# Recurrent layer of a decoder step: gate units issued behind the previous head's matrices, copied out by VectorE, silu in place

## The chip, the cores and the metric

The kernel runs on one core of a Trainium2 chip. The metric is the device time of one execution in microseconds (us). The core has five engines with queues of their own: TensorE (PE, matmuls, which land in eight PSUM banks), VectorE (DVE), ScalarE (ACT), GpSimd (POOL) and SyncE (SP, here the issuer of the DMAs). They meet at semaphores; each engine works through its own list strictly in order.

## The reference, cut to what matters

One inference step of a two-layer decoder, 512 prompt tokens and 32 sample tokens (8 sequences of 4), model width 1024, all float32. Layer 0 is a gated linear recurrence with 8 heads of 128, layer 1 is attention; each is followed by a mixture of experts. The change is in layer 0 alone:

```python
def hgrn2_mixer(hn, w_in, lb, gnorm_w, w_o, s0):
    proj = hn @ w_in                              # 1024 x 4096
    q, f, i, g = jnp.split(proj, 4, axis=-1)
    fg = lb + (1.0 - lb) * jax.nn.sigmoid(f)
    logf, k = jnp.log(fg), 1.0 - fg
    o, s_new = gla_chunked(heads(silu(q)), heads(k), heads(i), heads(logf), s0)
    o = rmsnorm(o, gnorm_w).reshape(B, T, A_WIDTH) * jax.nn.silu(g)
    return o @ w_o, s_new
```

`gla_chunked` carries a 128 x 128 state through the tokens: decayed products of q and k inside a chunk, q times the carried state, and the state's update from k and i. The gate `g` enters only at the very end, as `silu(g)` times the gain `gnorm_w`.

## The kernel before

The program is a row of stages with a barrier between them. `hgrn_block` is the stage of the change. It holds i as `hgrn_v` and g as `hgrn_g`, by tokens: five token tiles of 128, 128, 128, 128 and 32 rows. A **unit** is one projection into one PSUM bank:

- `v` units, ten of them (two halves of 512 columns by five token tiles), ahead of everything else;
- `g` units, the **gate units**, numbered 0 to 9 in the same way (half n // 5, token tile n % 5). Units 4 and 9 are the tiles of 32 rows. A unit of 128 rows is eight matmuls of 512 columns (L404), one of 32 rows is 32 matmuls of 128 columns (L407);
- `f` and `q` units of a head, by feature, eight matmuls each (L774); and for every second head an `s` unit (L407), f and q of the sample tokens for two heads, which ScalarE copies out (L522) and TensorE transposes (L833).

All units but `s` take banks 0 and 1 in turn, in the order in which they are issued. `begin(u)` lets TensorE wait until the unit that had the bank before has been read out. `f` is read out by ScalarE's sigmoid (L527, L529), `q` by its silu (L533, L534), a gate unit by its silu (L541).

The heads follow each other in software pipeline. For head h the engines do this:

- VectorE and ScalarE, function `elementwise` and `exponentials`: the logarithm (L546), a prefix sum (L632), and for seven levels i = 0 to 6 differences (L649, L650, L655), their exponential (ScalarE L560) and the products with q (VectorE L672) and with k (GpSimd L736, the last one L740, called kd here). Level i + 1's differences need level i - 1's products, so the three engines hand each level on to each other.
- TensorE, function `gla(h)`: transposes of kd (L787), six sets of masked products (L794, each read out by VectorE L682), the state's steps, and the output of the head into banks 7 and 6, the last of which are the matmuls of L817. It begins with waits for all products of head h. ScalarE's copy of the output (L569) is the first thing behind `gla(h)` and ahead of the next logarithm (L546), because in ScalarE's list `results(h)` stands before `exponentials(h + 1)`.

In TensorE's list the order is: f and q of head h, the gate units of head h, then `gla(h - 1)`. ScalarE's list has for head h: read out f and q, silu of the gate units, `results(h - 1)`, `exponentials(h)`. The split of gate units over the heads is a table:

```python
GATE_UNITS = [[("g", n // NT, n % NT) for n in range(*span)] for span in ((0, 2), (2, 3), (3, 4), (4, 5), (5, 6), (6, 7),
                                                                          (7, 8), (8, 8), (8, 10))]
```

So head 0 has two gate units, heads 1 to 6 one each, head 7 none, and two follow between `gla(6)` and `gla(7)`. VectorE multiplies all ten units of `hgrn_g` with the gain (L718) after `elementwise(7)` and ahead of `matrices(7)`, the reading out of `gla(7)`.

The weights of the gate come in two tiles of 2 MB, through a ring of three slots; the second one may be loaded once gate unit 4 is done, since it takes the first one's slot.

## Time and profile before

| | us |
|---|---|
| median of 3 runs | 1665.6 (1656.18 to 1666.4) |
| the profiled execution, whole | 1667.51 |
| its span, first to last instruction | 1665.8 |
| TensorE busy in the span | 1347.6 (81%) |
| VectorE, ScalarE, GpSimd busy | 744.7, 392.9, 170.4 |

The profiled execution took 1.7 us more than its span, and 1.9 us more than the median of the other runs. Busy time is a share over all stages; the stage of the change runs from about 36 to 463 us of the span, and its pipeline of heads from 101 to 461 us. Mean granted clock of TensorE is 0.897 of full speed.

### The profile page before, as it was taken

How to read it: one execution, taken by the hardware profiler on the slowest of the kernel's cores; microseconds unless marked ns; L12 is line 12 of the kernel's file. 1: busy time of each engine (PE TensorE's matmuls, PEld its weight loads, DVE VectorE, ACT ScalarE, POOL GpSimd, SP SyncE). 2: the span in 40 equal slices, each digit the busy share in tenths (PEclk: the TensorE clock that was granted, in tenths of full speed). 3: DMA queues.
4: the chain of work that ended last, by engine and by line, in shares of the span. 5: the costliest groups of instructions: out<-in, count | busy, mean ns of one | idle time of the engine just before them, and what ended most of it. 6: DMA issues, size and time to landing. Idle time of an engine off the chain costs nothing. (4 is left out here: it accounts for less than half of the span.)

```text
span 1665.8 us, 29086 instructions
## 1 busy us (share of the span) xinstructions
PE 1347.6 (81%) x11207; PEld 766.3 (46%) x11207; DVE 744.7 (45%) x1874; ACT 392.9 (24%) x1070; POOL 170.4 (10%) x242
## 2 busy tenths in 40 slices
PE   3998888888679999971999986678778689999880
PEld 2444555455445765541454543344444245765540
DVE  4314465446756331115110454688887156321115
ACT  2013333333321121112001120244444211121111
POOL 1002222222200100002000000100100000100002
PEclk9999999999789799995999988799899789799995
DMA  5140314112371699953131649999999771699924
GB/s 206 51 133 0 116 56 157 65 56 67 115 254 51 227 366 364 335 199 107 58 115 51 245 167 349 364 407 398 398 406 366 280 262 51 234 365 352 327 63 161
DMA packets 132156, 347.56 MB, mean 209 GB/s; under 512 B 22012, under 2 KB 51887, under 8 KB 123824
## 3 DMA queue, kind: packets, MB, share of 16 engines
q1 hardware_dynamic: 115652, 315.21, 52.3%
q0 software_dynamic: 4992, 17.83, 3.0%
q10 hardware_dynamic: 11372, 12.62, 2.4%
q8 instruction: 92, 1.51, 0.4%
q14 instruction: 48, 0.39, 0.1%
HBM read 302.09 MB, written 43.52 MB: 207 GB/s over the span
## 5 line engine op out<-in xcount | busy, mean ns | idle before, releaser
L404 PE MATMUL bank<-wring,xT 128*128 128x512 f32 x512 | 242.0, 632 | 24.6 <-ACT gla_fin L527 16.1
L404 PEld LDWEIGHTS bank<-wring,xT 128*128 128x128 f32 x512 | 102.2, 203 | 153.8 <-issue 132.5
L1304 PE MATMUL bank<-wring,xT 128*128 128x512 f32 x256 | 119.3, 619 | 2.0 <-DVE xT L1224 2.0
L774 PE MATMUL bank<-xT,wring 128*128 128x512 f32 x256 | 111.9, 595 | 0.0
L2301 DVE STREAM_TRANSPOSE wring<-wring 128x1024 f32<-128x1024 f32 x64 | 77.3, 1228 | 41.8 <-DMA wring<-cache_k 41.3
L2301 DVE STREAM_TRANSPOSE attn_q_xT<-attn_q_xT 128x1024 f32<-128x1024 f32 x64 | 77.0, 1227 | 32.2 <-DMA attn_q_xT<-cache_k 32.0
L1304 PEld LDWEIGHTS bank<-wring,xT 128*128 128x128 f32 x256 | 49.3, 199 | 59.4 <-issue 59.3
L682 DVE COPY_PREDICATED gla_att<-level_masks,bank 128x512 f32<-128x512 int32 x48 | 35.1, 730 | 92.2 <-PE bank L794 92.2
L774 PEld LDWEIGHTS bank<-xT,wring 128*128 128x128 f32 x256 | 48.1, 190 | 59.3 <-issue 59.3
L1937 PE MATMUL bank<-attn_q_xT,wring 128*128 128x512 f32 x128 | 56.9, 597 | 0.0
L794 PE MATMUL bank<-gla_qe,gla_ke 128*128 128x128 f32 x384 | 52.5, 295 | 4.7 <-DVE gla_att L682 4.7
L794 PEld LDWEIGHTS bank<-gla_qe,gla_ke 128*128 128x128 f32 x384 | 49.2, 206 | 7.7 <-DVE gla_att L682 7.0
L1511 DVE TENSOR_TENSOR hgrn_g<-hgrn_g,bank 128x128 f32<-128x128 f32 x32 | 7.8, 284 | 83.4 <-ACT hgrn_g L1460 83.4
L1511 DVE TENSOR_TENSOR attn_qo<-attn_qo,bank 128x128 f32<-128x128 f32 x32 | 7.8, 284 | 83.4 <-ACT attn_qo L1460 83.4
L560 ACT ACTIVATE gla_diff<-gla_diff 128x512 f32<-128x512 f32 (+1 forms) x48 | 30.3, 632 | 60.6 <-DVE gla_diff L650 51.5
L2156 PE MATMUL bank<-ident,attn_k 128*128 128x128 f32 x80 | 16.5, 330 | 34.5 <-DVE attn_k L2293 34.5
L2217 PE MATMUL bank<-wring,sa_at 128*32 128x512 f32 x224 | 38.4, 818 | 7.1 <-DMA wring<-cache_v 7.0
L329 PE MATMUL bank<-ident,attn_k 128*128 128x128 f32 (+1 forms) x40 | 6.5, 323 | 46.1 <-DVE attn_k L384 43.5
L732 POOL TENSOR_TENSOR gla_ke<-gla_k,gla_diff 128x544 f32<-128x544 f32 x8 | 10.8, 1345 | 297.8 <-ACT gla_diff L555 297.8
L2417 ACT ACTIVATE attn_k<-attn_k,pa_stat 128x128 f32<-128x128 f32 (+2 forms) x64 | 35.3, 555 | 25.0 <-DVE pa_stat L2284 25.0
L736 POOL TENSOR_TENSOR gla_ke<-gla_k,gla_diff 128x256 f32<-128x256 f32 x40 | 34.9, 871 | 42.3 <-ACT gla_diff L560 42.3
L1467 ACT ACTIVATE moe_norm_w<-bank 128x512 f32<-128x512 f32 x32 | 19.1, 597 | 84.6 <-PE bank L1615 84.6
(425 smaller groups left out, 2355.6 us busy)
## 6 DMA issues: line engine op xcount, KB each, us to landing
wring<-cache_k SPq DMA_DIRECT2D x64, 512.0 KB, 7.0
attn_q_xT<-cache_k SPq DMA_DIRECT2D x64, 512.0 KB, 8.0
xT<-cache_v SPq DMA_DIRECT2D x60, 512.0 KB, 7.7
wring<-cache_v SPq DMA_DIRECT2D x56, 512.0 KB, 6.3
moe_wd<-moe_w_down SPq DMA_DIRECT2D x20, 1024.0 KB, 13.8
wring<-moe_w_gate SPq DMA_DIRECT2D x18, 1024.0 KB, 13.0
wring<-moe_w_up SPq DMA_DIRECT2D x18, 1024.0 KB, 15.5
wring<-a_w_in SPq DMA_DIRECT2D x16, 1024.0 KB, 8.9
```

Of the source, the lines that this page charges most:

```text
L404: last = nc.tensor.matmul(bank[:, :], xT[:, c, cols(t)], w[:, c, :], start=(c == 0), stop=(c == DC - 1))
L560: nc.scalar.activation(diff[i % 2][:, 0:w], diff[i % 2][:, 0:w], ACT.Exp).then_inc(exp_ready, 1)
L682: nc.vector.copy_predicated(A[:, :, :], bcast(k.levelmask[:, i, :].bitcast(I32), 1, [P, PT, P]), k.ps[3 + i % 2][:, :].rearrange("p (c n) ...
L736: nc.gpsimd.tensor_tensor(blocks(KE[j][:, :], size)[:, :, lo], blocks(kk[:, 0:SEQ], size)[:, :, lo], blocks(diff[j % 2][:, 0:SEQ], size)[: ...
L774: last = nc.tensor.matmul(bank[:, :], lhsT, k.xT[:, c, 0:SEQ], start=(c == 0), stop=(c == DC - 1))
L794: last = nc.tensor.matmul(k.ps[3 + i % 2][:, part], KE[i][:, part], QE[i][:, part], start=True, stop=True)
L1304: last = nc.tensor.matmul(bank[:, :], k.xT[:, c, cols(t)], w[:, c, :], start=(c == 0), stop=(c == DC - 1))
L1467: nc.scalar.activation(self.YW[u][:, :], k.ps[5][:, :], ACT.Copy).then_inc(self.y_a, 1)
L1937: last = nc.tensor.matmul(k.ps[2 + h % 2][:, :], w[h // 4][:, c, (h % 4) * P:(h % 4 + 1) * P], self.q_xT[:, c, 0:SEQ], start=(c == 0), sto ...
L2217: last = nc.tensor.matmul(VALUE[n][QUAD * r:QUAD * (r + 1), :], AT[:, p, :], keys.values(v_s)[:, r, n * HB:(n + 1) * HB], start=(g == 0), ...
L2301: nc.vector.transpose(page, page).then_inc(keys_turned, 1)
L2417: last = nc.scalar.activation(part, part, ACT.Exp, bias=s[:, x, 2 + c:3 + c], accum_out=s[:, x, 4 + c:5 + c])
```

## The change

It does four things. In TensorE's list `gla(h - 1)` moves ahead of the gate units of head h. A gate unit is read out of its bank by VectorE, with a plain copy (`gate_out`) that stands inside `elementwise(h)`, behind the products of level i = 4; ScalarE's silu then runs in place on the copy in SBUF, one head later (`gate`), and VectorE's product with the gain (`gate_norm`) follows `elementwise` of that later head, unit by unit, instead of all ten in one go. And the table gives head 6 no gate unit and head 7 three: units 7, 8 and 9.

```diff
-GATE_UNITS = [[("g", n // NT, n % NT) for n in range(*span)] for span in ((0, 2), (2, 3), (3, 4), (4, 5), (5, 6), (6, 7),
-                                                                          (7, 8), (8, 8), (8, 10))]
+GATE_UNITS = [[("g", n // NT, n % NT) for n in range(*span)] for span in ((0, 2), (2, 3), (3, 4), (4, 5), (5, 6), (6, 7), (7, 7), (7, 10))]
 GATE_TILE_AT = [0, 4]
+GATES_AFTER = 4
...
             order += [("f", h), ("q", h)] + GATE_UNITS[h]
-        order += GATE_UNITS[HEADS]
...
                 def gate(u):
-                    done, bank = units[u]
                     _, i, t = u
-                    act.wait_ge(proj_done, done)
-                    for n, (src, dst) in enumerate(token_parts(k.ps[bank], g, i, t)):
-                        last = nc.scalar.activation(dst, src, ACT.Silu)
-                    last.then_inc(g_out, 1)
+                    act.wait_ge(*evacuated[u])
+                    part = g[0:rows(t), t, i * HB:(i + 1) * HB]
+                    nc.scalar.activation(part, part, ACT.Silu).then_inc(g_ready, 1)
...
                 for h in range(HEADS):
                     evacuate_qf(h)
-                    for u in GATE_UNITS[h]:
-                        gate(u)
                     if h:
+                        for u in GATE_UNITS[h - 1]:
+                            gate(u)
                         results(h - 1)
                     exponentials(h)
-                for u in GATE_UNITS[HEADS]:
+                for u in GATE_UNITS[HEADS - 1]:
                     gate(u)
...
+                def gate_out(u):
+                    done, bank = units[u]
+                    dve.wait_ge(proj_done, done)
+                    for src, dst in token_parts(k.ps[bank], g, u[1], u[2]):
+                        last = nc.vector.tensor_copy(dst, src)
+                    last.then_inc(g_out, 1)
+
+                def gate_norm(u):
+                    _, i, t = u
+                    dve.wait_ge(g_ready, NT * i + t + 1)
+                    gv = g[0:rows(t), t, i * HB:(i + 1) * HB].rearrange("p (h n) -> p h n", n=P)
+                    nc.vector.tensor_tensor(gv, gv, bcast(gnorm[0:rows(t), :], 1, [rows(t), 4, P]), ALU.mult)
...
                                                     blocks(diff[j % 2][:, 0:SEQ], size)[:, :, up], ALU.mult).then_inc(q_lev, 1)
+                        if i == GATES_AFTER:
+                            for u in GATE_UNITS[h]:
+                                gate_out(u)
...
                 for h in range(1, HEADS):
                     matrices(h - 1)
                     elementwise(h)
-
-                for i in range(2):
-                    for t in range(NT):
-                        dve.wait_ge(g_out, NT * i + t + 1)
-                        gv = g[0:rows(t), t, i * HB:(i + 1) * HB].rearrange("p (h n) -> p h n", n=P)
-                        nc.vector.tensor_tensor(gv, gv, bcast(gnorm[0:rows(t), :], 1, [rows(t), 4, P]), ALU.mult)
+                    for u in GATE_UNITS[h - 1]:
+                        gate_norm(u)
                 matrices(HEADS - 1)
+                for u in GATE_UNITS[HEADS - 1]:
+                    gate_norm(u)
...
+                    if h:
+                        gla(h - 1)
                     for u in GATE_UNITS[h]:
                         by_token(u, w_gate)
-                    if h:
-                        gla(h - 1)
-                for u in GATE_UNITS[HEADS]:
-                    by_token(u, w_gate)
                 gla(HEADS - 1)
```

What the change does to the lists is seen best in the built program. First TensorE, from f and q of head 1 to f and q of head 2, before. The names: `wring` is the ring of weights, `xT` the normed input, a number behind `bank` is the PSUM bank; `gla_inv4` holds kd, L817 is the last line of `gla`.

```order
L774 MATMUL bank0<-xT,wring2 128x512 x8
L774 MATMUL bank1<-xT,wring2 128x512 x8
L404 MATMUL bank0<-wring0,xT 128x512 x8
L787 MATMUL bank5<-ident,gla_inv4 128x128 x4
...
L817 MATMUL bank6<-gla_s0_0,gla_qb 32x128 x8
L407 MATMUL bank2<-wring1,xT 32x128 x32
L774 MATMUL bank1<-xT,wring1 128x512 x8
L774 MATMUL bank0<-xT,wring1 128x512 x8
```

The same stretch of TensorE's list after the change, where L785 is the former L774, L798 the former L787 and L828 the former L817:

```order
L785 MATMUL bank0<-xT,wring2 128x512 x8
L785 MATMUL bank1<-xT,wring2 128x512 x8
L798 MATMUL bank5<-ident,gla_inv4 128x128 x4
...
L828 MATMUL bank6<-gla_s0_0,gla_qb 32x128 x8
L404 MATMUL bank0<-wring0,xT 128x512 x8
L407 MATMUL bank2<-wring1,xT 32x128 x32
L785 MATMUL bank1<-xT,wring1 128x512 x8
L785 MATMUL bank0<-xT,wring1 128x512 x8
```

The gate unit (L404) has moved from ahead of `gla(0)` to behind it, and keeps bank 0; q of head 2, the last row, still follows it in bank 0.

Second, VectorE's list in the last head, from the products of level 4 to the reading out of `gla(7)`, before:

```order
L672 TENSOR_TENSOR gla_qe<-gla_q,gla_diff 128x16x16
L649 TENSOR_TENSOR gla_diff<-gla_b 128x4x64
L650 TENSOR_TENSOR gla_diff<-gla_b 128x4x64
L672 TENSOR_TENSOR gla_qe<-gla_q,gla_diff 128x8x32
L655 TENSOR_TENSOR gla_diff<-gla_b 128x512
L655 TENSOR_TENSOR gla_diff<-gla_b 128x32
L672 TENSOR_TENSOR gla_qe<-gla_q,gla_diff 128x4x64
L675 COPY gla_qb<-gla_qs 128x8x4
L718 TENSOR_TENSOR hgrn_g<-hgrn_g,row_gains 128x512 x4
L718 TENSOR_TENSOR hgrn_g<-hgrn_g,row_gains 32x512
...
L682 COPY_PREDICATED gla_att<-level_masks,bank 128x512 x6
```

The same after the change (L682 is the former L672, L695 the former L682, L659, L660 and L665 the former L649, L650 and L655):

```order
L682 TENSOR_TENSOR gla_qe<-gla_q,gla_diff 128x16x16
L621 COPY hgrn_g<-bank 128x512 x2
L621 COPY hgrn_g<-bank 32x128 x4
L659 TENSOR_TENSOR gla_diff<-gla_b 128x4x64
L660 TENSOR_TENSOR gla_diff<-gla_b 128x4x64
L682 TENSOR_TENSOR gla_qe<-gla_q,gla_diff 128x8x32
L665 TENSOR_TENSOR gla_diff<-gla_b 128x512
L665 TENSOR_TENSOR gla_diff<-gla_b 128x32
L682 TENSOR_TENSOR gla_qe<-gla_q,gla_diff 128x4x64
L688 COPY gla_qb<-gla_qs 128x8x4
L695 COPY_PREDICATED gla_att<-level_masks,bank 128x512 x6
```

The ten products with the gain are gone from ahead of the reading out, and six copies out of PSUM stand in the middle of the levels.

Third, TensorE's end of the pipeline, from f and q of head 7 on, before:

```order
L774 MATMUL bank<-xT,wring 128x512 x16
L787 MATMUL bank<-ident,gla_inv 128x128 x4
...
L817 MATMUL bank<-gla_s_0,gla_qb 32x128 x8
L404 MATMUL bank<-wring,xT 128x512 x8
L407 MATMUL bank<-wring,xT 32x128 x32
L787 MATMUL bank<-ident,gla_inv 128x128 x4
```

and after:

```order
L785 MATMUL bank<-xT,wring 128x512 x16
L798 MATMUL bank<-ident,gla_inv 128x128 x4
...
L828 MATMUL bank<-gla_s_0,gla_qb 32x128 x8
L404 MATMUL bank<-wring,xT 128x512 x16
L407 MATMUL bank<-wring,xT 32x128 x32
L798 MATMUL bank<-ident,gla_inv 128x128 x4
```

Between the last two `gla` stand three gate units instead of two.

## Rows read from the trace of the kernel before

**Rows 1.** Windows view, the pipeline of heads; busy us per engine, TensorE's clock, DMA.

```profile
101.00:461.30 360.30, 306.14 (x1504) 182.97 (x1500) 186.19 (x322) 127.84 (x251) 86.61 (x72) 0.91 0.27 89
```

**Rows 2.** Timeline of TensorE, heads 2 and 3; start, duration, in brackets idle before.

```profile
192.91 10.19 PE L404 MATMUL bank<-wring,xT 128*128 128x512 f32 x16 [1.58 <-ACT gla_fin L527]
202.94 0.60 PE L787 MATMUL bank<-ident,gla_inv 128*128 128x128 f32 x4
...
216.59 14.00 PE L774 MATMUL bank<-xT,wring 128*128 128x512 f32 x32
236.91 3.46 PE L407 MATMUL bank<-wring,xT 128*32 128x128 f32 x64 [6.32 <-ACT gla_fin L527]
```

**Rows 3.** Timelines of ScalarE, VectorE and GpSimd after `gla(1)`.

```profile
216.70 0.60 ACT L569 ACTIVATE hgrn_v<-bank 128x512 f32<-128x512 f32 x1 [12.27 <-PE bank L817]
...
230.68 0.41 DVE L672 TENSOR_TENSOR gla_qe<-gla_q,gla_diff 128x256 f32<-128x256 f32 x1
...
235.09 1.33 POOL L740 TENSOR_TENSOR gla_inv<-gla_k,gla_diff 128x544 f32<-128x544 f32 x1 [0.88 <-ACT gla_diff L560]
```

**Rows 4.** Timeline of ScalarE, copies of a head's output: heads 0, 5, 6, 7.

```profile
172.53 0.60 ACT L569 ACTIVATE hgrn_v<-bank 128x512 f32<-128x512 f32 x1 [12.28 <-PE bank L817]
...
384.23 0.60 ACT L569 ACTIVATE hgrn_v<-bank 128x512 f32<-128x512 f32 x1 [12.28 <-PE bank L817]
...
419.39 0.60 ACT L569 ACTIVATE hgrn_v<-bank 128x512 f32<-128x512 f32 x1 [12.30 <-PE bank L817]
...
461.34 0.60 ACT L569 ACTIVATE hgrn_v<-bank 128x512 f32<-128x512 f32 x1 [19.99 <-PE bank L817]
```

**Rows 5.** Timeline of TensorE, gate units 8 and 9 behind `gla(6)`.

```profile
419.29 7.13 PE L404 MATMUL bank<-wring,xT 128*128 128x512 f32 x16
426.35 1.96 PE L407 MATMUL bank<-wring,xT 128*32 128x128 f32 x64
```

**Rows 6.** Timeline of VectorE, copies of `v` units out of PSUM.

```profile
97.51 0.69 DVE L617 COPY hgrn_v<-bank 128x512 f32<-128x512 f32 x1 [6.17 <-PE bank L404]
99.43 1.18 DVE L617 COPY hgrn_v<-bank 32x128 f32<-32x128 f32 x4 [1.22 <-PE bank L407]
```

**Rows 7.** Timelines of TensorE, ScalarE and VectorE in head 0.

```profile
128.72 13.90 PE L774 MATMUL bank<-xT,wring 128*128 128x512 f32 x32
...
117.19 0.19 ACT L534 ACTIVATE gla_q<-bank 128x32 f32<-128x32 f32 x1
...
129.53 1.28 ACT L546 ACT_TABLE_LOAD   x1
130.83 0.66 ACT L546 ACTIVATE gla_fin<-gla_fin 128x544 f32<-128x544 f32 x1
...
142.71 0.41 DVE L672 TENSOR_TENSOR gla_qe<-gla_q,gla_diff 128x256 f32<-128x256 f32 x1
```

**Rows 8.** TensorE behind short waits (timeline), and its clock (windows: ..., clock, DMA, GB/s).

```profile
52.23 15.70 PE L404 MATMUL bank<-wring,xT 128*128 128x512 f32 x32 [2.30 <-DVE hgrn_v L617]
...
1106.29 1.95 PE L2183 MATMUL bank<-wring,sa_q 128*32 128x128 f32 x64 [1.64 <-DVE sa_red L2310]
...
192.90:199.10 6.20, 6.19 (x8) 2.57 (x9) 0.00 (x0) 2.02 (x4) 3.07 (x2) 0.50 0.00 0
```

**Rows 9.** Timelines of TensorE and VectorE, `gla(6)` and `gla(7)`.

```profile
404.05 1.09 PE L787 MATMUL bank<-ident,gla_inv 128*128 128x128 f32 x4 [5.93 <-POOL gla_inv L740]
439.27 1.08 PE L787 MATMUL bank<-ident,gla_inv 128*128 128x128 f32 x4 [10.96 <-POOL gla_inv L740]
...
448.65 5.53 PE L794 MATMUL bank<-gla_qe,gla_ke 128*128 128x128 f32 x32 [4.67 <-DVE gla_att L682]
...
437.30 10.66 DVE L718 TENSOR_TENSOR hgrn_g<-hgrn_g,row_gains 128x512 f32<-128x512 f32 x10
```

**Rows 10.** Source view of L718 (ns min/median/max), DMA view (KB each, us to landing).

```profile
L718 DVE TENSOR_TENSOR hgrn_g<-hgrn_g,row_gains x10: 672/674/2397, 437.3 to 447.3; 128x512 f32<-128x512 f32 x8, 32x512 f32<-32x512 f32 x2
...
wring<-a_w_in SPq DMA_DIRECT2D x8, 1024.0 KB, 9.1
```

More of the change, by code:

```diff
@@ L482, in hgrn_block @@
         proj_done, s_copied, s_turned = k.sem("proj_done"), k.sem("sample_qf_copied"), k.sem("sample_qf_turned")
-        v_out, qf_out, g_out = k.sem("v_evacuated"), k.sem("qf_evacuated"), k.sem("g_evacuated")
+        v_out, qf_out, g_out, g_ready = k.sem("v_evacuated"), k.sem("qf_evacuated"), k.sem("g_evacuated"), k.sem("g_ready")
         evacuated = {}
```

## Prediction, made before the changed kernel had run

> **What bounds the kernel now.** I read the windows first, then the chain of work around one head. The pipeline of heads takes 360.3 us, and TensorE is busy for 306.1 of them [rows 1]; it is the busiest engine by far, and idles 54 us. The timeline of TensorE shows where: after f and q of head 3 it stands still for 6.32 us until ScalarE's sigmoid has read f out of its bank (L527), because the gate unit wants that bank; only then come the gate unit and `gla(2)` [rows 2]. ScalarE is late since the exponentials of head 2 stand ahead of that sigmoid. So the loop of a head is serial: end of `gla`, levels, sigmoid, gate unit, next `gla`.
>
> I count from a mark M, the start of ScalarE's copy L569, which is released by the last matmul of `gla`. After M = 216.70 the products of level 4 end at 231.09, M + 14.4; kd starts at 235.09 and ends at M + 19.7 [rows 3]. With kd everything is there that `gla` needs: in the one head without a gate unit, `gla(6)` starts at 404.05, which is M + 19.8 behind the mark of 384.23 [rows 4, 9]. `gla` itself lasts 13.8 us when the clock is at full speed (202.94 to 216.70 [rows 2, 3]), and 15.3 when TensorE comes to it from a wait (404.05 to 419.39 [rows 4, 9]). Before, a gate unit of 7.1 to 10.2 us [rows 2, 5] lay between M + 19.8 and `gla`. The marks run from 172.53 for head 0 to 461.34 for head 7 [rows 4], 41.3 us a head.
>
> **The change, part by part.** *Gate units behind `gla`.* TensorE now goes from `gla(h - 1)` straight into the gate unit of head h, then s, f and q of head h + 1, while VectorE, ScalarE and GpSimd work through the levels. Prices at full clock: f or q 7.0 (two in 14.00 [rows 2]), gate unit 7.1 [rows 5] (7.0 here), small gate unit or s unit 1.9 [rows 5]. TensorE starts 0.1 ahead of M. The wait for the sigmoid goes: f of head h is read out while `gla(h - 1)` runs.
>
> *What is late next* is the bank. q of head h + 1 takes the bank of the gate unit of head h, which VectorE now frees behind level 4. A copy of 128 x 512 out of PSUM takes 0.69, the four copies of a small unit 1.18 [rows 6]. The bank is free at M + 14.4 + 0.7 = M + 15.1, or M + 15.6 for the small unit.
>
> Heads by their lists, TensorE's time from mark to mark:
> - Marks 1 to 2 and 3 to 4 (gate, f, q): f ends at M + 13.9, q waits to 15.1 and ends at 22.1; `gla` 13.8 makes 35.9 each.
> - Marks 0 to 1 and 4 to 5 (gate, s, f, q): f ends at 15.8, so no wait; q ends at 22.8, the transpose of L833 adds 0.3; 36.9 each.
> - Mark 2 to 3 (small gate, s, f, q): f ends at 10.7, q waits to 15.6, 4.9 idle. Behind such waits the clock falls to the lower level, 1.2 GHz: 0.50 from 192.9 to 199.1 [rows 8]. The price is 1.7 (15.70 for work that takes 14.0, behind a wait of 2.30 [rows 8, 2]) to 3.1 (the gate unit of 10.19 against 7.1 [rows 2, 5]); I take 2.4. Sum 15.6 + 7.0 + 2.4 + 0.3 + 13.8 = 39.1.
> - Mark 5 to 6 (f, q, no gate): limited by the levels as before, 419.39 - 384.23 = 35.2 [rows 4].
> - Mark 6 to 7: gate units 7 and 8 end at M + 13.9. Unit 9 needs unit 7's bank, free at 15.1, and ends at 17.05. VectorE stands in the middle of its levels until then, and its four copies end at 18.25: the levels resume 3.85 later than at M + 14.4. `gla(7)` starts at 19.8 + 3.85 = 23.65, from a wait, so 15.3: 39.0.
>
> Together 258.9 from mark 0 to mark 7, against 288.8 before: 29.9 less.
>
> *Head 0.* `gla(0)` comes ahead of gate unit 2, and ScalarE no longer holds the logarithm back for two silus of gate units. Before, L546 loads its table at 129.53 and starts at 130.83; now the table (1.28) follows the silu of q, which ends at 117.38, so the logarithm starts at 118.7 and all levels 12.1 earlier [rows 7]. Level 4's product ends at 143.1 - 12.1 = 131.0, the first gate bank is free at 131.7. TensorE is through with both gate units at about 128.8 (f of head 1 started at 128.72), so it now waits 2.9 us where it did not; f and q take 14.0 plus 1.7 for the clock, to 147.4. `gla(0)` ends at 161.2 instead of 172.5: 11.3 less. All in all 41.2 less, with mark 7 near 420.1.
>
> *The end.* The ten products with the gain (10.66 us on VectorE) no longer stand ahead of the reading out of `gla(7)`, for which TensorE waited 4.67 [rows 9]; that is inside the 39.0. Three of them now follow `matrices(7)` at 0.67 each [rows 10], 2.0 in all. `matrices` ends with L706, for which TensorE has long issued what it needs: it still has the whole output of the head to do (L810 to L817), which covers them; without that cover they cost 2.0.
>
> *Work that is merely moved.* ScalarE's silus in place stand between the silu of q and the transposed kd's copy; `gla` needs that copy only behind its six sets of products, which are the larger part of its 13.8 us, so one or two silus are covered. The second gate tile's load waits for gate unit 4, now done 1.9 behind mark 2, and TensorE asks for it ahead of `gla(3)`, at about M + 25; a load takes 9.1 to land [rows 10], twice that still fits. SyncE's later loads and stores move with the marks. The number of table loads stays.
>
> *Two places where a price has two ends.* The waits of 1.2 us ahead of q (two heads), and of 1.15 ahead of unit 9: behind 1.64 us of waiting, 64 matmuls took 1.95, the full-clock time of rows 5, and behind 2.30 us the clock had fallen [rows 8]. I take no loss; if it falls there, 1.7 to 3.1 for each. The Trainium skill ("TensorE: Matmul & The Clock Gate", "What's actually happening") has the activity monitor free-running, not started by the kernel, so that the same wait may or may not cost the clock. By it two or three such waits would give back some 5 us more; the rows with 1.64 and 2.30 neither confirm nor rule that out.
>
> The products with the gain now run just as GpSimd does kd and its two next operations. Ten took 10.66 where ten times 0.67 is 6.7, and one took 2.397 [rows 9, 10]: I read that as waiting for GpSimd. If they hold kd back in turn, by 0.67 to 1.4 per head, `gla` could start at M + 20.5 + 1.4 = 21.9, still ahead of q's end at 22.1; I take nothing. The Trainium skill ("SBUF — State Buffer", "Who interferes with whom") says that a VectorE instruction with two SBUF inputs and a GpSimd instruction that reads SBUF block each other fully, whichever starts first. That speaks against putting them side by side; by it kd is late in six heads, but behind q.
>
> **The rivals.** *The levels become the bound.* With the copy (0.7) and blocked products of up to 2.4 us ahead of or beside kd, kd ends at M + 19.7 + 0.7 + 2.4 = 22.8, and with the port taken twice at 24. Five heads lose 1 to 2 us: 5 to 10 us given back, 1629 to 1634. For it: L718's 2.397. Against: L740 is the first of GpSimd's three operations, and VectorE's products with the gain come behind all its own levels, so mostly GpSimd is first.
>
> *The clock gives back what the order gains.* TensorE goes cold at all short waits: two heads, unit 9 and a longer spell in head 0 and mark 2 to 3: 3 x 3.1 + 1.4 + 0.7 = 11, so 1636.
>
> *Slower: the bank of the gate unit.* TensorE is strictly in order, and q of head h + 1 waits for VectorE's copy; behind q stands `gla(h)`, behind that the next levels. A head costs copy's end + 7.0 + 13.8. It equals the former 41.3 when the copy ends at M + 20.5, 5.4 later than computed; at M + 23 every head costs 2.5 us more than before, and the five heads concerned with the other terms unchanged give about 1675. That would need level 4 itself to be that late; nothing in rows 3 moves it, since its inputs come from ScalarE and GpSimd, which lose nothing ahead of it.
>
> *The change does not do what it says:* some wait that I missed keeps TensorE where it was, and only head 0 and the end gain: 1650. The built order speaks against it.
>
> **How the numbers follow.** The profiled execution was 1667.5; less 41.2 gives 1626.3. Against the median of the runs, 1665.6, it gives 1624.4, and I forecast 1624. Nothing behind the stage depends on absolute time; the stages behind it move forward as a whole. The runs before spread over 10 us, so a change of under 1% can't be told from none. Chances: forecast (1615 to 1629) 0.62; levels 0.12; clock 0.14; only part of it, 1640 to 1650, 0.06; slower 0.03; better than computed, below 1615 (a fast draw like 1656.18, or less cold clock), 0.03. The range takes in the first four cases but the tails: 1612 to 1640. Faster by over 1% is below 1649: 0.92; within 1% 0.05; slower 0.03.
>
> **What would show it.** Right: marks 35 to 39 us apart; TensorE goes on into the gate unit without a wait behind `gla`; a wait of about 1 us ahead of q, released by L621; `gla(7)` without a wait for VectorE in its middle; mark 7 near 420. Wrong: `gla` released by kd in most heads, gate units or q at 10 us, or L621 at M + 20.

## The result, and the profile after

The changed kernel takes 1617.55 us (median of 5 runs, 1615.37 to 1626.92) against 1664.99 us before (1656.18 to 1666.4, 5 runs). The ratio is 0.9723, with a 95% interval of 0.9694 to 0.9752. The forecast was 1624 with a range of 1612 to 1640, so time and direction came as forecast. The middle was 6.5 too high; that is within what the medians of one kernel do here, since the same changed kernel has 1624.55 in its second session (e11, below), where the gain over before is 40.4 and not 47.4.

The profiled execution of the changed kernel took 1626.92 us (span 1625.2, mean granted clock 0.909), 40.6 less than the profiled one before. First the marks, from the timeline of ScalarE: heads 0, 2, 3, 5 and 7, the rows that answer to [rows 4]. L566 is the former L569.

```profile
158.36 0.60 ACT L566 ACTIVATE hgrn_v<-bank 128x512 f32<-128x512 f32 x1 [11.22 <-PE bank L828]
...
230.69 0.60 ACT L566 ACTIVATE hgrn_v<-bank 128x512 f32<-128x512 f32 x1 [11.75 <-PE bank L828]
...
270.07 0.60 ACT L566 ACTIVATE hgrn_v<-bank 128x512 f32<-128x512 f32 x1 [10.24 <-PE bank L828]
...
342.40 0.60 ACT L566 ACTIVATE hgrn_v<-bank 128x512 f32<-128x512 f32 x1 [10.23 <-PE bank L828]
...
417.54 0.60 ACT L566 ACTIVATE hgrn_v<-bank 128x512 f32<-128x512 f32 x1 [13.66 <-PE bank L828]
```

With those of heads 1, 4 and 6 (194.92, 305.85 and 378.86) the seven distances are, beside the forecast:

| us | head 0 | 0-1 | 1-2 | 2-3 | 3-4 | 4-5 | 5-6 | 6-7 | mark 7 |
|---|---|---|---|---|---|---|---|---|---|
| before | 172.53 | 44.17 | 37.42 | 42.66 | 43.57 | 43.88 | 35.16 | 41.95 | 461.34 |
| forecast | 161.2 | 36.9 | 35.9 | 39.1 | 35.9 | 36.9 | 35.2 | 39.0 | 420.1 |
| changed | 158.36 | 36.56 | 35.77 | 39.38 | 35.78 | 36.55 | 36.46 | 38.68 | 417.54 |

Mark 7 came 43.8 earlier, and the span is shorter by 40.6. What follows the mark took 1204.5 before and 1207.7 here. That part is the same program, and in all the profiled executions of this study it took between 1198.0 and 1210.9 (two executions of one and the same kernel: 1198.0 and 1207.5). Its granted clock is 0.89 in both kernels, and TensorE is busy in it for 970.5 us before and 971.4 us after. The 3 us are left open, as a draw of those stages.

Second, the pipeline's windows, the view of [rows 1], over the stretch of before, which now holds 44 us of the next stage too, and over the pipeline alone:

```profile
101.00:461.30 360.30, 327.87 (x1608) 194.82 (x1607) 210.87 (x421) 133.91 (x269) 88.02 (x82) 0.95 0.35 117
...
101.00:417.60 316.60, 292.96 (x1499) 176.71 (x1497) 187.30 (x338) 125.34 (x245) 86.44 (x72) 0.97 0.31 101
```

TensorE idled 54.2 of 360.3 us before; now it idles 23.6 of 316.6. So 30.6 of the 43.7 us are idle time that is gone. The other 13.2 are its own work, 306.1 to 293.0 us. Of that 0.9 is work that now lies ahead of 101 us, since the pipeline starts 1.0 earlier; the other 12.2 are the same matmuls in less time: the clock in the stretch rose from 0.91 to 0.97.

Third, the waits view of TensorE from 101 to 418 us, with all that it lists there (total, times, longest):

```profile
PE bank L798 <- POOL gla_inv L751: 12.2, 2, 6.3
PE bank L785 <- DVE hgrn_g L621: 10.2, 4, 5.0
PE bank L407 <- DVE hgrn_g L621: 1.1, 1, 1.1
```

None of the waits for the sigmoid (L527, L529) or for the samples' copy (L522) is left; that copy stood for 8.5 us in the same view of before, which the prediction didn't name, though its lists rightly have no such wait. What stands there now is the pair that the prediction named: the copy L621 ahead of q, and kd (L751, the former L740) in the last two heads. Last, TensorE's timeline around `gla(1)` and `gla(2)` and at the last head. This answers to [rows 2] and [rows 9]; L785 is the former L774, L798 the former L787.

```profile
130.76 14.00 PE L785 MATMUL bank<-xT,wring 128*128 128x512 f32 x32 [2.85 <-DVE hgrn_g L621]
...
201.78 7.03 PE L785 MATMUL bank<-xT,wring 128*128 128x512 f32 x16
209.96 7.13 PE L785 MATMUL bank<-xT,wring 128*128 128x512 f32 x16 [1.15 <-DVE hgrn_g L621]
...
246.22 10.13 PE L785 MATMUL bank<-xT,wring 128*128 128x512 f32 x16 [5.01 <-DVE hgrn_g L621]
...
362.59 1.08 PE L798 MATMUL bank<-ident,gla_inv 128*128 128x128 f32 x4 [6.30 <-POOL gla_inv L751]
363.68 8.02 PE L805 MATMUL bank<-gla_qe,gla_ke 128*128 128x128 f32 x48
...
393.90 1.96 PE L407 MATMUL bank<-wring,xT 128*32 128x128 f32 x64 [1.15 <-DVE hgrn_g L621]
401.79 1.09 PE L798 MATMUL bank<-ident,gla_inv 128*128 128x128 f32 x4 [5.94 <-POOL gla_inv L751]
...
402.89 7.49 PE L805 MATMUL bank<-gla_qe,gla_ke 128*128 128x128 f32 x48
```

The forecast waits were 1.2, 4.9, 2.9 (head 0) and 1.15 (ahead of unit 9); the rows have 1.15, 5.01, 2.85 and 1.15. The six sets of masked products of `gla(7)` (L805 at 402.89) have no wait for VectorE in their middle.

### The profile page after: what moved, and what is told of

Its sections match the earlier page's. It is cut to its first block and busy times, and to the rows that moved or that the text cites. A ratio compares the mean times of both kernels' runs of the same rounds, so it can differ in the third digit from the quotient of the medians.

```text
span 1625.2 us, 29095 instructions
## 1 busy us (share of the span) xinstructions
PE 1337.0 (82%) x11207; PEld 763.4 (47%) x11207; DVE 745.8 (46%) x1890; ACT 391.1 (24%) x1064; POOL 168.7 (10%) x242
## 5 line engine op out<-in xcount | busy, mean ns | idle before, releaser
L404 PE MATMUL bank<-wring,xT 128*128 128x512 f32 x512 | 227.8, 602 | 5.0 <-PEq L359 4.4
L404 PEld LDWEIGHTS bank<-wring,xT 128*128 128x128 f32 x512 | 96.9, 192 | 124.6 <-issue 123.2
L785 PE MATMUL bank<-xT,wring 128*128 128x512 f32 x256 | 115.6, 609 | 10.2 <-DVE hgrn_g L621 10.2
L1313 PE MATMUL bank<-wring,xT 128*128 128x512 f32 x256 | 120.4, 624 | 2.0 <-DVE xT L1233 2.0
L785 PEld LDWEIGHTS bank<-xT,wring 128*128 128x128 f32 x256 | 49.0, 194 | 73.3 <-issue 59.8
L1313 PEld LDWEIGHTS bank<-wring,xT 128*128 128x128 f32 x256 | 49.8, 201 | 60.1 <-issue 60.0
L695 DVE COPY_PREDICATED gla_att<-level_masks,bank 128x512 f32<-128x512 int32 x48 | 35.1, 731 | 61.3 <-PE bank L805 61.3
L805 PE MATMUL bank<-gla_qe,gla_ke 128*128 128x128 f32 x384 | 51.8, 293 | 0.0
L805 PEld LDWEIGHTS bank<-gla_qe,gla_ke 128*128 128x128 f32 x384 | 48.7, 205 | 2.9 <-DVE gla_att L695 2.4
L2192 PE MATMUL bank<-wring,sa_q 128*32 128x128 f32 x1024 | 32.2, 279 | 6.3 <-DVE sa_red L2319 6.3
```

The lines of the kernel that those rows point to most:

```text
L404: last = nc.tensor.matmul(bank[:, :], xT[:, c, cols(t)], w[:, c, :], start=(c == 0), stop=(c == DC - 1))
L695: nc.vector.copy_predicated(A[:, :, :], bcast(k.levelmask[:, i, :].bitcast(I32), 1, [P, PT, P]), k.ps[3 + i % 2][:, :].rearrange("p (c n) ...
L785: last = nc.tensor.matmul(bank[:, :], lhsT, k.xT[:, c, 0:SEQ], start=(c == 0), stop=(c == DC - 1))
L805: last = nc.tensor.matmul(k.ps[3 + i % 2][:, part], KE[i][:, part], QE[i][:, part], start=True, stop=True)
L1313: last = nc.tensor.matmul(bank[:, :], k.xT[:, c, cols(t)], w[:, c, :], start=(c == 0), stop=(c == DC - 1))
L2192: last = nc.tensor.matmul(out.rearrange("p (r x) -> p r x", r=GROUP), Q[b % 2][:, h, i, :], keys.K[s % 2][:, :, at:at + QUAD], start=(i == ...
```

## The experiments

There are twelve runs: nine edited kernels, two of them twice, and the changed kernel again. The theory in all of them: TensorE is the bound in the heads with a gate unit, and the time from mark to mark is its own work plus the wait for the bank that VectorE's copy frees. Unless said otherwise "the marks" are those of the profiled execution, and "rest" is what follows mark 7.

### The two halves of the change, each without the other

**e1_order_back** keeps the copies by VectorE and the late silu, and puts the gate units ahead of `gla` again (and unit 7 back to head 6):

```diff
+                    for u in GATE_UNITS[h]:
+                        by_token(u, w_gate)
                     if h:
                         gla(h - 1)
-                    for u in GATE_UNITS[h]:
-                        by_token(u, w_gate)
```

> Undone: gate units stand ahead of the previous head's matrices again (units 7 / 8, 9 to heads 6 / 7, since three there would need a bank that is not yet free); VectorE's copies, silu in place and the single products with the gain stay. Theory (the order is what pays): the loop is serial again and the copy adds a wait of q for its bank from about M + 7 to M + 15.1, so a head takes q's end 22.1 + 2.4 for the clock + gate unit 7 + matrices 13.8, about 45 us, 40 for the small unit; mark 7 between 462 and 472 us instead of 417.5, time 1662 to 1672, no faster than the kernel before. Rival (the copies by VectorE and the spread products with the gain are what pays, the order little): mark 7 below 440, time below 1640.

Measured: 1675.68 us, ratio to before 1.0036 (1.0007 to 1.0064). Mark 7 is at 467.63, the distances are 37.1 to 46.6. **e5_silu_by_scalar** is the other half: the new order, but ScalarE's silu reads the gate unit out of its bank, behind the last exponential and ahead of the next head's sigmoid (unit 7 is with head 6, as in e1).

```diff
-                    part = g[0:rows(t), t, i * HB:(i + 1) * HB]
-                    nc.scalar.activation(part, part, ACT.Silu).then_inc(g_ready, 1)
+                    for src, dst in token_parts(k.ps[bank], g, u[1], u[2]):
+                        last = nc.scalar.activation(dst, src, ACT.Silu)
+                    last.then_inc(g_out, 1)
```

> The new order in TensorE's list stays, but ScalarE reads the gate units out with silu as before, at the first place where it can without holding up the levels: behind the last exponential of the head (one table load more per head); units 7 / 8, 9 to heads 6 / 7. Theory (the order pays only if the bank is freed in the middle of the levels): the gate's bank is free at M + 18.3 + 1.3 + 0.6 = M + 20.2, q waits for it and ends at 27.2 to 30, a head takes 41 to 44 us, mark 7 near 463 us, about the kernel before (461.3); time 1655 to 1668. Rival (the order alone pays, whoever reads out): marks 36 to 37 us apart, mark 7 below 430.

Measured: 1673.15 us, ratio 1.0047 (1.0015 to 1.008), mark 7 at 461.12, distances 42.5 to 44.5 but for the last (35.0). Mark 7 lies where it was expected in both (462 to 472, and near 463); the whole times came 4 and 5 us above their ranges. Neither half alone is faster than before; by the ratios both are slower, by 0.4 and 0.5%. The timelines of TensorE say why. In order, e1 with f and q around 180 us, then e5 behind its gate unit at 207.58:

```profile
180.24 9.02 PE L785 MATMUL bank<-xT,wring 128*128 128x512 f32 x16 [6.26 <-DVE hgrn_g L621]
189.20 7.03 PE L404 MATMUL bank<-wring,xT 128*128 128x512 f32 x16
196.07 0.60 PE L798 MATMUL bank<-ident,gla_inv 128*128 128x128 f32 x4
```

```profile
207.58 7.13 PE L404 MATMUL bank<-wring,xT 128*128 128x512 f32 x16
...
227.91 10.02 PE L777 MATMUL bank<-xT,wring 128*128 128x512 f32 x16 [6.33 <-ACT hgrn_g L539]
```

In e1 a bank filled early waits for a copy in the middle of the levels (6.26), and the gate unit still stands between the levels and `gla`. In e5 the gate unit is out of the way, but its bank comes free only behind all exponentials (6.33). It takes the order and the reading out together.

**e6_levels_padded** was meant to lengthen the levels of the changed kernel. By a mistake the kernel that ran was that of e5, line for line, without any padding. Its expectation therefore speaks of a kernel that did not run, and its time says nothing on the levels:

> The change, with six products of 136 columns added on VectorE behind the copies of every head: 1.2 to 1.8 us of useless work in the levels, which delays kd but not the bank. Theory (kd comes 1.9 us before TensorE wants it in the gated heads): marks 0 to 5 as before within 0.3, marks 5 to 6 and 6 to 7 longer by the padding, mark 7 later by 2.4 to 3.6. Rival (the levels are the bound): every head longer by the padding, mark 7 later by 10 us or more.

Measured: 1673.69 us in one run, mark 7 at 461.15, which is e5 again (461.12). The padding that was meant is in e9 and e10.

### Where the copy stands

The price of the bank is set by one number, behind which level the copies stand.

```diff
-GATES_AFTER = 4
+GATES_AFTER = 2
```

**e4_copies_level2** has 2 in that line, **e8_copies_level6** has 6.

> Only the place of VectorE's copies moves, from behind level 4 to behind level 2 (M + 10.9). Theory (after the change TensorE is bound by the bank in heads 0, 2, 3, 4 and by its own work elsewhere): no wait ahead of q in marks 1 to 2 and 3 to 4 (34.6 instead of 35.8), mark 2 to 3 falls from 39.4 to about 34.4, head 0's wait of 2.85 goes (mark 0 at about 155.5 instead of 158.4), and the last head loses 3 us, since VectorE then waits in its levels for units 8 and 9: mark 7 at about 410.5 instead of 417.5. Rival (the levels have become the bound): kd comes no earlier, marks stay at 35.8, mark 7 at 417 or, with the last head, above.

> Only the place of the copies moves, to behind level 6 (M + 18.2). Theory (a gated head costs copy's end + 7.0 + clock + 13.8): q starts at M + 18.9, heads 1 to 5 take 41.3 to 43 us each, mark 7 near 448, time near 1648: most of the gain is gone though the order is the new one. Rival (bank not the limit): mark 7 below 425.

Measured: with 2, 1612.68 us, ratio 0.9678 (0.965 to 0.9706), mark 7 at 407.68; with 6, 1654.25 us, ratio 0.9921 (0.9888 to 0.9953), mark 7 at 444.89. TensorE's timelines, e4 first, then e8:

```profile
229.45 7.13 PE L785 MATMUL bank<-xT,wring 128*128 128x512 f32 x16
238.10 7.13 PE L785 MATMUL bank<-xT,wring 128*128 128x512 f32 x16 [1.52 <-DVE hgrn_g L621]
246.39 0.63 PE L798 MATMUL bank<-ident,gla_inv 128*128 128x128 f32 x4 [1.05 <-issue]
```

```profile
204.93 7.13 PE L404 MATMUL bank<-wring,xT 128*128 128x512 f32 x16
211.90 7.03 PE L785 MATMUL bank<-xT,wring 128*128 128x512 f32 x16
223.58 9.21 PE L785 MATMUL bank<-xT,wring 128*128 128x512 f32 x16 [4.65 <-DVE hgrn_g L621]
```

Two levels later cost 4.65 - 1.15 = 3.5 us of wait in the two heads that have a gate unit of 128 rows and no `s` unit, and 2.1 us of clock on q (9.21 against 7.13): 5.6, and the distances 1-2 and 3-4 grew by 5.6 and 5.1. In 0-1 and 4-5, where the `s` unit stands in between, the wait is 2.6 and q takes 8.8, and these distances grew by 4.6 and 4.5. This is the prediction's slower rival at work: its formula, a head costs the copy's end + 7.0 + 13.8, gives 39.4 for a copy that ends at M + 18.6 (223.58 - 205.03 = 18.55); measured for this head is 41.36, the difference being the clock's, about 2. So the formula holds with one correction: behind a wait of that size q takes 9.2 and not 7.0. With it the break-even is not the M + 20.5 of the prediction but about M + 18.5, where this copy ends: 41.4 is the former average of 41.3. That the kernel is still 0.8% faster than before comes from other places: mark 7 is 16.5 earlier, 8.6 of that in head 0, 5.8 in the five heads with a gate unit (which had 42.3 on average before) and 2.1 in the last two. Two levels earlier takes the waits of 1.15 away: 1-2 and 3-4 go from 35.77 to 34.36, with no wait left in them, and head 0 gains 3.2 (mark 0 at 155.14). The small-gate head goes from 39.38 to 34.12: its wait for the copy shrinks from 5.01 to 1.52 and costs no clock. There a new wait shows, 1.05 behind q, which the view calls "issue" and which ends when kd is done. So in that head the levels are the bound now (of its gain of 5.3 us, 3.1 is the clock's price behind the wait, which in e11 is 1.5); in 1-2 kd ends at M + 20.1 and TensorE asks for it at M + 20.6.

In the last head it went the other way: 40.85 against 38.68. VectorE's timeline of that head in e4:

```profile
377.64 0.68 DVE L621 COPY hgrn_g<-bank 128x512 f32<-128x512 f32 x1
380.76 0.69 DVE L621 COPY hgrn_g<-bank 128x512 f32<-128x512 f32 x1 [2.44 <-PE bank L404]
382.68 1.18 DVE L621 COPY hgrn_g<-bank 32x128 f32<-32x128 f32 x4 [1.22 <-PE bank L407]
```

Behind level 2 VectorE comes to the copies before TensorE has made the units, and stands still in the middle of its levels for 2.44 and 1.22 us.

### The table, and the products with the gain

**e2_table_even** gives unit 7 back to head 6, the rest as changed; **e3_norms_at_once** does all ten products with the gain after `elementwise(7)` again.

```diff
-((0, 2), (2, 3), (3, 4), (4, 5), (5, 6), (6, 7), (7, 7), (7, 10))
+((0, 2), (2, 3), (3, 4), (4, 5), (5, 6), (6, 7), (7, 8), (8, 10))
```

```diff
-                    for u in GATE_UNITS[h - 1]:
+                for us in GATE_UNITS:
+                    for u in us:
                         gate_norm(u)
                 matrices(HEADS - 1)
-                for u in GATE_UNITS[HEADS - 1]:
-                    gate_norm(u)
```

> One part undone: gate unit 7 with head 6 and units 8, 9 with head 7, as in the kernel before; all else as after the change. Theory (three units kept for the last head cost): marks 5 to 6 take 35.8 instead of 36.5, marks 6 to 7 lose VectorE's wait for unit 9, levels late by 1.5 instead of 3 us, 36.8 to 37.2 instead of 38.7; mark 7 at 415.0 to 415.5 instead of 417.5. Rival (the third unit fills a wait and pays): mark 7 at 419 or more. Whole time within noise of after, 1613 to 1627.

> One part undone: all ten products with the gain in one go ahead of the reading out of the last head's matrices. Theory: they cost TensorE a wait in the last matrices as before (4.67 there), now from later on; VectorE is through with them 10.7 us behind the levels, at M6 + 33, and mark 7 comes 13.4 behind that as before: 46.5 instead of 38.7 for the last head, mark 7 at about 425, time 5 to 9 above after. Rival (the products spread over the heads hold up kd there): heads 1 to 6 each 0.5 to 1 us shorter, so that mark 7 stays below 421.

Measured: e2 1623.42 us, ratio 0.9739 (0.9703 to 0.9775), mark 7 at 414.69, where the changed kernel has 417.54. Its distances 5-6 and 6-7 are 36.11 and 36.06, together 72.2; the changed kernel has 75.1, and 74.1 in its second session. The three units of the last head are a cost of 2 to 3 us, not a gain; the whole time cannot tell it. (The expectation had 36.8 to 37.2 for the last distance; it came at 36.06.) e3 1628.16 us, ratio 0.9762 (0.9726 to 0.9798), mark 7 at 423.6, so 6.1 later; the last head is 6.8 longer (45.48 against 38.68), the others together 0.7 shorter. Its timelines of VectorE and TensorE have the wait of before again:

```profile
399.13 10.66 DVE L628 TENSOR_TENSOR hgrn_g<-hgrn_g,row_gains 128x512 f32<-128x512 f32 x10
```

```profile
410.58 5.86 PE L804 MATMUL bank<-gla_qe,gla_ke 128*128 128x128 f32 x32 [5.28 <-DVE gla_att L695]
```

### Is TensorE the bound, or the levels?

The nearest rival by chance was that the levels, with kd at their end, are the bound already. **e9_pad3** and **e10_pad8** put three and eight small products of 128 x 136 on VectorE behind the gate copies, in every head. They touch no bank and only make the levels longer.

```diff
                         if i == GATES_AFTER:
                             for u in GATE_UNITS[h]:
                                 gate_out(u)
+                            for _ in range(3):
+                                ch(nc.vector.tensor_tensor(mid4[:, :], k.restart[:, 0:TOK // 4], k.restart[:, 0:TOK // 4], ALU.mult))
```

> Three small products of 128 x 136 (0.40 us each, 1.2 in all, each waiting for the one before) are put on VectorE behind the gate copies, in every head. They lengthen the levels and touch no bank. Theory: TensorE is bound by its own work and the bank, and kd has about 1.9 us of slack in heads with a gate unit of 128 rows, so marks 0 to 5 stand within 0.3 us of the changed kernel's distances (36.6, 35.8, 39.4, 35.8, 36.6), and only the heads without that cover, 5 to 6 and 6 to 7, grow, by 0.8 to 1.3 each: mark 7 at 419 to 420.5. Rival (the levels are the bound): every distance grows by about 1.2, mark 7 near 426.

> The same with eight such products, 3.2 us in every head. Theory: kd is late now by 3.2 - 1.9 = 1.3 in marks 1 to 2 and 3 to 4 (with 0.6 to 1.5 more where the start from a wait costs clock), by 0.4 in 0 to 1 and 4 to 5, not in the small-gate head (2 to 3), and by the whole 3.2 in 5 to 6 and 6 to 7. Sum of mark distances 10 to 14 us above the changed kernel's 259.2, mark 7 at 428 to 432, and TensorE's transposes (L801) wait for kd in four heads. Rival (the levels are the bound already): seven times 3.2, 22 us, mark 7 near 440.

The changed kernel ran on the same chip as the yardstick, **e11_change_again**:

> The changed kernel itself, unedited, as the yardstick for the two padded kernels and the best version on the same chip: 1613 to 1625, mark 7 at 417 to 418.

Measured: e9 1622.33, e10 1635.36 (one run each), e11 1624.55 (1616.3 to 1633.63, ratio 0.9754, 0.9695 to 0.9814). The distances:

| us | 0-1 | 1-2 | 2-3 | 3-4 | 4-5 | 5-6 | 6-7 | mark 7 |
|---|---|---|---|---|---|---|---|---|
| e11, the change | 36.56 | 35.78 | 37.82 | 35.78 | 36.56 | 35.97 | 38.16 | 415.25 |
| e9, 1.2 us more | 36.55 | 35.78 | 39.37 | 35.78 | 36.56 | 36.64 | 39.12 | 417.4 |
| e10, 3.2 us more | 37.04 | 36.66 | 38.71 | 36.68 | 36.69 | 38.33 | 41.59 | 423.81 |

The last two distances of e9 grew by 0.7 and 1.0 against e11, where 0.8 to 1.3 was written (against the changed kernel's first session by 0.2 and 0.4). But 1.2 us of padding in every head moves no distance with a gate unit by more than 0.01, but for 2-3, where q's clock differs (below). The rival, which wanted 1.2 in each, falls. GpSimd's timeline shows how far the larger dose goes; kd at mark 1, the changed kernel first (M = 194.92), then e10 (M = 195.15):

```profile
213.64 1.38 POOL L751 TENSOR_TENSOR gla_inv<-gla_k,gla_diff 128x544 f32<-128x544 f32 x1 [0.88 <-ACT gla_diff L557]
```

```profile
216.54 1.38 POOL L753 TENSOR_TENSOR gla_inv<-gla_k,gla_diff 128x544 f32<-128x544 f32 x1 [0.88 <-ACT gla_diff L557]
```

kd ends at M + 20.10 in the changed kernel and at M + 22.77 in e10; TensorE asks for it at M + 22.0. So there is 1.9 of slack, and e10 overshoots it by 0.8: the distances 1-2 and 3-4 grew by 0.9, and TensorE waits for kd in four heads, as expected. The total grew less than expected (mark 7 at 423.81, where 428 to 432 was written): 3.2 us of padding make kd only 2.7 later, and the last two distances grew by 2.4 and 3.4 against e11, by 1.9 and 2.9 against the changed kernel's first session. That kd moves by less than what is put ahead of it has a reason in the rows, below.

### The best version

**e7_level2_even_late** joins what e4 and e2 gained and mends what e4 lost: copies behind level 2, unit 7 with head 6, and the two units of head 7 copied behind its last level.

```diff
-                        if i == GATES_AFTER:
+                        if i == GATES_AFTER and h < HEADS - 1:
                             for u in GATE_UNITS[h]:
                                 gate_out(u)
...
+                    if h == HEADS - 1:
+                        for u in GATE_UNITS[h]:
+                            gate_out(u)
```

> Three places bettered at once: copies behind level 2 in heads 0 to 6, unit 7 back with head 6, and the copies of units 8 and 9 behind the last level of head 7, where no bank waits for them. By the theory mark 0 at 155.5, heads 34.6, 34.4 and 36.5 us, the last one 35.1: mark 7 at 403 to 404, 14 us below the change, time 1603 to 1606. By the rival (levels are the bound) no earlier than 413.

Measured: 1609.66 us, ratio 0.9664 (0.9632 to 0.9697), mark 7 at 401.38. **e12_best_again** is the same kernel beside the changed one on one chip:

> The kernel of e7_level2_even_late again, beside the changed kernel on one chip. By the marks it is 16 us ahead of the changed kernel at mark 7; earlier in whole time it was 8 ahead by the medians of different sessions. If the whole gain of the marks reaches the end: 1601 to 1606; if the later stages' clock takes part of it: 1607 to 1612.

Measured: 1603.21 us (1601.06 to 1609.78), ratio to before 0.964 (0.9597 to 0.9682), against 1624.55 for the change in the same session. Mark 7 is at 401.30, 14.0 us ahead of e11; the other 7 us between the medians lie in the rest (1198.0 against 1208.7 in the profiled executions), which the edit doesn't touch: the same kernel had a rest of 1207.5 in e7, where its whole time came 4 us above the range expected. TensorE's timeline at its last head shows that nothing of the gate is waited for any more, only kd:

```profile
365.55 7.13 PE L404 MATMUL bank<-wring,xT 128*128 128x512 f32 x16
...
385.49 1.09 PE L801 MATMUL bank<-ident,gla_inv 128*128 128x128 f32 x4 [10.92 <-POOL gla_inv L754]
```

## Why the prediction was right

**The wait that goes, and what is late next.** Right, and measured at the rows named: the waits for L527 and L529 (24.1 us in the waits view of before) are gone, and q waits 1.15 for L621, with 1.2 predicted. e4 and e8 move that copy and the heads follow it.

**The heads by their lists.** Six of seven distances are within 0.35 of the forecast. That their sum fits to 0.3 (259.2 against 258.9) is in part luck: 5-6 came 1.3 too long, the other six together 1.0 too short. e1 and e5 show that the two halves work only together, which the prediction's sum assumed and did not say.

**The small-gate head.** 39.38 against 39.1. The wait is 5.01 (4.9), the clock cost 3.1 (2.4 taken, 1.7 to 3.1 given). In e11 the same wait cost 1.5. One of the prediction's signs of being wrong, q at 10 us, shows in this head (10.13), but in no other, and its sum had room for it here.

**Mark 5 to 6.** The one clear miss among the heads: 35.2 forecast as "limited by the levels as before", 36.46 measured (35.97 in e11). The step that failed is the term itself, taken over from before unchanged. kd ended at M + 20.1, 0.4 later than before, though no copy stands in that head: behind an idle of 0.46 the first difference of a pair fell beside GpSimd's product (0.95 for 0.42), where before it was the second. What made it late, no run shows. And `gla(6)` behind the wait took 16.3 from its start to the mark, where the row of before gave 15.3 and e11 has 15.8: the clock's share of such a start differs from run to run.

**Mark 6 to 7.** 38.68 against 39.0, and two misses cancel in it. The copies ended at M + 18.2, as forecast (18.25), but `gla(7)` started at M + 22.9 and not 23.65, since the levels took up 0.7 of the delay; and `gla(7)` behind its wait took 15.75, not 15.3. Of the distance, three units instead of two are 2 to 3 us (e2), which the sum contained without naming it.

**Head 0.** Forecast 161.2, measured 158.36. The wait came (2.85 against 2.9), its clock cost of 1.7 did not: f and q behind it took 14.00, full-clock time. That was a draw and no error of the term: behind the same wait (2.85 to 2.88) f and q took 14.00 in four executions (the changed kernel twice, e9, e10) and 15.70 in three (e1, e2, e3), which is the 1.7. The other 1.0 is that the pipeline started 1.0 earlier (L785 at 100.06, before at 101.03), also a draw: in e1 it started at 98.34.

**Work that is merely moved.** Right. Products with the gain: seven in the shadow of TensorE's work beside the levels, and the three behind `matrices(7)` end at 416.67, ahead of mark 7; L628's source view has a median of 678 ns and one of 1823. kd beside such a product took 1.38, without one 1.33 (the last head), so the price that the prediction bounded at 0.67 to 1.4 a head is 0.05. All ten at once cost 6.1 at mark 7 (e3).

At mark 1 such a product ran from 213.15 to 213.83 and kd from 213.64, so the two overlapped for 0.2 us. The Trainium skill ("SBUF — State Buffer", "Who interferes with whom") has the block fall on both sides, whichever starts first. At mark 1 the trace shows less: a full block would have cost kd the 0.2, and it took 0.05 more. At mark 0 the trace agrees, on both sides. GpSimd's timeline there:

```profile
177.09 1.39 POOL L751 TENSOR_TENSOR gla_inv<-gla_k,gla_diff 128x544 f32<-128x544 f32 x1 [0.88 <-ACT gla_diff L557]
178.45 2.33 POOL L758 TENSOR_TENSOR gla_vm<-hgrn_v,batch_mask 32x1024 f32<-32x1024 f32 x1
```

Two products with the gain stand there, of 2.42 us together: the second, begun while kd ran, took 1.82 for 0.67 and ended at 179.03, and GpSimd's next operation, begun in the middle of it, took 2.33, where it takes 1.89 in the seven other heads.

**The rivals.** The levels as the bound: excluded by e9, with 1.9 us of slack; but with the copies behind level 2 (e4) they are the bound in the small-gate head, and in 1-2 the slack is down to 0.5. The clock giving back: it did so at the waits of 5 and 6 us, never at 1.15, and at 2.85 in three of seven executions, not in the changed kernel's two. So 9.3 of this rival's 11 us, for the three waits of 1.15, came nowhere; the 0.7 in the small-gate head came, head 0's share did not. Slower by the gate's bank: the mechanism is real (e8 loses 27 us at mark 7 to it), its place was two levels off. Its 1675 leaves the other terms as they were before; with the forecast's own (head 0 and the last two distances), five heads of 43.8 in place of the forecast's 184.7 together are 34 us above 1624, so 1658. The change not doing what it says: the waits view excludes it.

**The sum.** 41.2 was forecast for the stage and 43.8 came at mark 7: 1.7 clock in head 0 and 1.0 from an earlier start, both draws. The profiled span gained 40.6. So the mechanism and the sum of the heads were right, and the nearness of the whole time, with medians of one kernel 7 us apart, says little more than that.

## What to carry to other kernels

When a result sits in a bank until an engine reads it, price two places: which work the bank's next owner holds up, and where the reader stands in its own chain; moving the unit without moving the reader, or the reader without the unit, gained nothing here, and both together 2.8%. Ask for every read-out in the middle of a chain whether its producer is surely done by then: behind level 2 the copies gained 1.4 to 5.3 us in four heads (the largest with 1.5 to 3.1 of clock in it), and lost 2.2 in the one head whose units were not ready. And a slack is measured best by padding: two doses, one below and one above what the timeline says.

## What the runs showed of the hardware

**The price of one and the same wait differs from run to run.** q of head 3 comes behind a wait of 5.01 us in six executions, and takes 7.03 at full clock. It took 10.13 in the first of them (the row at 246.22 above), 10.01 in e2 and 8.83 in e3. TensorE's timelines of the other three, in order the changed kernel in its second session, e10 and e9:

```profile
246.49 8.57 PE L785 MATMUL bank<-xT,wring 128*128 128x512 f32 x16 [5.01 <-DVE hgrn_g L621]
```

```profile
247.35 9.46 PE L787 MATMUL bank<-xT,wring 128*128 128x512 f32 x16 [5.01 <-DVE hgrn_g L621]
```

```profile
245.46 10.13 PE L787 MATMUL bank<-xT,wring 128*128 128x512 f32 x16 [5.01 <-DVE hgrn_g L621]
```

The windows view of the changed kernel's two executions over the same 3 us of q, first session and then second, has the granted clock at 0.50, the lower level of 1.2 GHz, in the one and back towards full speed in the other:

```profile
248.00:251.00 3.00, 3.00 (x5) 1.35 (x4) 1.62 (x4) 2.34 (x4) 2.12 (x3) 0.50 0.80 324
```

```profile
248.00:251.00 3.00, 3.00 (x6) 1.21 (x5) 1.89 (x5) 2.08 (x3) 2.12 (x2) 0.76 0.98 385
```

So the cost of the wait of 5.01 us is 1.5 to 3.1 us here. It is nothing behind 1.15 (six waits in the changed kernel's two executions) and 1.7 behind the 2.30 of [rows 8]. Behind 2.85 to 2.88 it is nothing in four executions and 1.7 in three; e2's row beside the 14.00 of the changed kernel:

```profile
129.28 15.70 PE L785 MATMUL bank<-xT,wring 128*128 128x512 f32 x32 [2.88 <-DVE hgrn_g L621]
```

In e8 waits of 2.59 and of 8.50 cost the same: q took 8.83 and 8.78. The length of the wait alone does not give the price. The Trainium skill ("TensorE: Matmul & The Clock Gate", "What's actually happening") has the activity monitor free-running, so that its phase against the program varies; by it a draw like this is expected, and these rows agree.

**VectorE's chain absorbs part of what is put into it.** VectorE's timeline of the changed kernel at mark 1, with the copy between two levels:

```profile
207.66 0.43 DVE L659 TENSOR_TENSOR gla_diff<-gla_b 128x256 f32<-128x256 f32 x1
208.00 0.97 DVE L660 TENSOR_TENSOR gla_diff<-gla_b 128x256 f32<-128x256 f32 x1
...
209.23 0.68 DVE L621 COPY hgrn_g<-bank 128x512 f32<-128x512 f32 x1
209.83 0.88 DVE L659 TENSOR_TENSOR gla_diff<-gla_b 128x256 f32<-128x256 f32 x1
210.63 0.41 DVE L660 TENSOR_TENSOR gla_diff<-gla_b 128x256 f32<-128x256 f32 x1
```

Counted from the mark, the pair behind the copy ends at M + 16.1; in the kernel before, without a copy there, at M + 15.8. So 0.68 us of copy cost 0.33. In each pair one difference takes twice the 0.42 of the other, while GpSimd's product of the level runs; I read that as VectorE waiting for GpSimd, as in the prediction, and the copy partly runs in that time. This reading is argued from the timelines, no experiment takes GpSimd's product away.

**Open:** the rest behind mark 7 varies by 13 us between executions of the same instructions, and no experiment was made on it. The expectations written for the marks held better than those for the whole times; besides those named, e8 came at 444.89 and 1654.25, where 448 and 1648 were written, and e11's mark 7 2 us earlier than the 417 to 418 expected.
